# DeltaNet phase: the keys' norms from the diagonal of the key product, the values' convolution among the stages, the key-query product first

## Chip, cores and metric

The kernel runs on one core of a Trainium2 chip. The metric is the device time of one execution in microseconds (us). The engines are called PE (TensorE), DVE (VectorE), ACT (ScalarE), POOL (GpSimd) and SP (SyncE, which here only issues DMAs). Each engine works through its own instruction list; semaphores order the engines against each other. A difference under about 0.5% (9.6 us) can't be told from no change in a measurement of this kernel.

## What is computed

One layer of a hybrid encoder over 1024 prompt rows and 32 sample rows. The change lies wholly in mixer A, a gated delta rule over 8 heads. Cut to what matters:

```python
act = silu(causal_conv(u))                        # 4 taps, for q, k and v
q = l2norm(act_q) * DKA ** -0.5                   # x * rsqrt(sum(x * x) + 1e-6)
k = l2norm(act_k)
kk = einsum('nbhid,nbhjd->nbhij', kc, kc)
M = where(strict, beta * kk * decay_in, 0.0)      # decay_in = exp(G_i - G_j), 1 on the diagonal
sol = triangular_solve(M + eye, [beta * v, beta * exp(G) * k], lower=True)
qk = einsum('nbhid,nbhjd->nbhij', qc, kc) * decay_in
# then the recurrence over blocks: u = u_v - w_k S; o = q_dec S + qk u; S = S g_last + k_dec^T u
```

## The kernel before

The phases run one after the other: entry, DeltaNet (`phase_deltanet`, about 98 to 790 us of the trace), attention, merge, residual, dispatch, experts. Only the second is touched.

**Fill.** The projections of q, k, v and z (the gate) of all heads are products of the input with weights, each split into a high and a low part, so that a product is three matmuls (lines 142 to 144). One product of one head ("job") is 3 parts of 8 steps; a step is three matmuls. PE takes these steps as fill between the small products of the delta rule: `run(fill, n)` emits n of them. Weights of a job go through three engines: SP loads `wraw` (one buffer, so the DMA of job w waits for the split of job w-1), ACT makes the high part (`high`, line 625, right after it has taken the last part of a job), DVE (`low`, line 1065) or POOL (line 811) subtracts to get the low part. PE waits for the split at a job's first step.

**Order.** For h from -1 to 7 there is one pass of the loop, which works on two heads: the recurrence of head h, and the preparation of head a = h + 1. First come nine slots (one for each block of 128 rows of head h), then twelve stages, in the order of the tuple `A2`, for the inverse of the triangular matrix of head a. In a slot PE does the product of WE with the state S (line 1004), half of the slot's fill, the update with u (lines 1013 and 1014), the other half, and then a part of `prep(a)`. The DVE does u (line 1276), a part of its own `prep(a)`, S (line 1280), and another part. ACT does a part of its `prep(a)`, the evacuation of the block's output to `obuf`, and whatever products have become ready (`take`). Each `yield` in a `prep` ends a part. In pass -1 there is no recurrence.

**Fill steps.** Passes 0 to 5 have 96: 6 in each slot, 54 in all, then 3, 4, 3, 4, ... after the twelve stages. Passes -1 and 6 have 60 (5 and 4 in a slot). In passes 0 to 5 a job ends after 12, 36, 60 and 84 steps. In pass -1 it is after 24 and 48, in pass 6 after 12, 36 and 60.

**Preparation before** (slot numbers): PE: norms of the keys (`SK`: 18 matmuls of the squares with ones, 36 PE instructions, line 907) and key product (`KK`, line 865) in 2, norms of the queries (`SQ`) in 3, transposed decayed product (`T_ET`) in 4, transposed keys (`T_K`) in 7. ACT: tap 0 of the queries in 0, SiLU and square of the keys in 1, exponential of the decay matrix Dm in 2, SiLU and square of the queries in 3, square root and copies of the 32-wide diagonal blocks of ET to `blk` (line 692) in 4, tap 0 of the values in 5, keys and the block inverses RT and R in 8. DVE: taps 1 to 3 of the keys in 0, query taps in 1, 2 and 3, Dm in 1, `col` (1/norm of the keys, lines 1090 to 1094) and the split of one job's weights in 2, ET = KK * Dm in 3, transposition of the blocks in 4, scaling and N in 5, elimination (14 steps, lines 1051 and 1052) in 6 and 7, transposing back in 7, the three value taps (line 1033) in 8.

**Stages before**: BT, B, T_V (transposed values), B2, W, TT, T_O (output of head h), Q, QK (key-query product), TX, WK, UV. After each, `run(fill, ...)`. Some of the lines that matter:

```python
after_stage = {"BT": 2, "W": 3}        # DVE splits these jobs' weights behind these stages
# PE                                   # ACT, for i, stage in enumerate(A2):
if name == "B2":                       #   if stage == "B": evacuate_halves(a, "B", B)
    evacuated(pe, a, "BT")             #                    silu(a, VB)
    evacuated(pe, a, "B")              #   for k in range(subs_done(h, done), subs_done(h, now)):
    stage(a, "B2", mul2(A1T, B), HB2)  #       take(k)      # and high() behind a job's last part
```

Stage BT on PE waits for RT on ACT, which waits for the DVE's transposes of the blocks (semaphore `x_done`). B2 waits for the evacuations of BT (DVE) and B (ACT).

Of the kernel before, what the change touches and what calls it, by code (L numbers as in the profile page):

```python
# [17 lines left out]
ALU = mybir.AluOpType  # L18
# [379 lines left out]
def phase_deltanet(nc, c):  # L398
# [38 lines left out]
    A2 = ("BT", "B", "T_V", "B2", "W", "TT", "T_O", "Q", "QK", "TX", "WK", "UV")  # L437
# [26 lines left out]
    for h in range(-1, HA):  # L464
        a = h + 1
        order = ([] if a == HA else ["SK", "KK", "SQ", "T_ET", "T_K"]) + \
                [s for s in A2 if (a < HA or s == "T_O") and (h >= 0 or s != "T_O")]
        for s in order:
            for g in range(NGRP):
                if (s == "SK" and g != 0) or (s == "SQ" and g != 1):  # L470
                    continue
                use[h if s == "T_O" else a, s, g] = count[g]
                count[g] += 1

    with ExitStack() as ctx:
# [17 lines left out]
        A1T, Q, bv, sqk, sqq = UV[:, 0:TILES * HB2], UV[:, TILES * HB2:PAD], ET, kt, N  # L493
# [69 lines left out]
        with nc.Block() as block:  # L563
# [53 lines left out]
            def _(act):  # L617
# [35 lines left out]
                def tap(a, b):  # L653

                    act.wait_ge(s["pj_taken"], 2 + NJ * (jobs.index((a, b)) + 1))
                    if a > 0:
                        act.wait_ge(full[NGRP - 1], use[a - 1, "QK", NGRP - 1] + 1)
# [10 lines left out]
                def square(a, b):  # L668

                    act.wait_ge(s["actv"], 3 * a + (1 if b == KB else 2))  # L670
                    act.activation((sqk if b == KB else sqq)[:, :], f[b][:, :], ACT.Square).then_inc(s["sq"], 1)

                def prep(a):
# [4 lines left out]
                    square(a, KB)  # L678
# [16 lines left out]
                    yield  # L695
                    if a > 0:
# [62 lines left out]
                for h in range(-1, HA):  # L759
# [16 lines left out]
                    for i, stage in enumerate(A2):  # L776
                        if a < HA:
                            if stage == "B":
                                evacuate_halves(a, "B", B)
                                silu(a, VB)  # L780
                            if stage == "TT":
                                evacuate_corners(a)
                            if stage == "Q":
# [10 lines left out]
                            if stage == "QK" and a + 1 < HA:  # L794
# [41 lines left out]
            def _(pe):  # L836
# [63 lines left out]
                def norms(a, name, g, sq, n):  # L900

                    pe.wait_ge(s["sq"], 2 * a + n)
                    if use[a, name, g] > 0:
                        pe.wait_ge(free[g], use[a, name, g])
                    for t in range(TILES):
                        for rows in HALVES:
                            mm = pe.matmul(stg[g][rows, t:t + 1], tl(sq, t)[:, rows], c.consts[:, C_ONE, 0:1], start=True, stop=True)
                    mm.then_inc(full[g], 1)
# [1892 lines left out]
```

## Time and profile before

| | us |
|---|---|
| median of three runs | 1916.19 (1912.34 to 1922.93) |
| the profiled execution | 1919.02 |
| its span, first to last instruction | 1917.2 |
| PE busy, DVE busy, ACT busy | 1718.0, 1073.7, 768.4 |
| mean granted TensorE clock | 0.951 of 2.4 GHz |

The prediction uses the page's busy shares, the busy time by stretches, the table of who waited for whom, and the timeline. In the timeline a PE row's duration overlaps the next row's (matmuls are pipelined), so costs on PE are taken from start to start.

### The profile page before, as it was taken

The page shows a single profiled execution, that of the slowest core. Times are in us where ns is not written, and L with a number is a line of the kernel's source. Part 1 is how long each engine was busy: PE and PEld are TensorE (multiplying, and loading weights), DVE is VectorE, ACT ScalarE, POOL GpSimd, SP SyncE. Part 2 cuts the span into 40 slices and gives each one's busy share as a digit, 9 for nine tenths or more (in the row PEclk, how much of TensorE's full clock was granted, in tenths as well). Part 3 has the DMA queues.
Part 4 walks back from the last instruction along what each step waited for, and adds up shares of the span by engine and source line. Part 5 has one row for each costly group of instructions (what it writes and reads, how often), then busy time and mean ns, then how long its engine had stood idle before and what let it go on. Part 6 is the DMA issues. An engine that isn't in the chain of part 4 may idle for free. (4 is left out here: it accounts for less than half of the span.)

```text
span 1917.2 us, 32170 instructions
## 1 busy us (share of the span) xinstructions
PE 1718.0 (90%) x12253; PEld 1479.6 (77%) x12254; DVE 1073.7 (56%) x2257; ACT 768.4 (40%) x1473; POOL 150.5 (8%) x143
## 2 busy tenths in 40 slices
PE   5798999999999989899998899999979946999990
PEld 2597899999989989788884699998967834666660
DVE  5555747557584765354445211134349975677676
ACT  3455554645556454254444222222021113444444
POOL 0100000000000000000000000000000002434340
PEclk8898999999999999999999999999999966999995
DMA  9311021120202111212117321113153246988866
GB/s 335 136 60 49 23 74 38 49 73 14 74 23 75 37 49 39 94 40 81 57 70 275 124 68 67 45 57 100 34 176 144 110 172 231 320 258 287 230 186 214
DMA packets 69030, 219.80 MB, mean 115 GB/s; under 512 B 8580, under 2 KB 14364, under 8 KB 64804
## 3 DMA queue, kind: packets, MB, share of 16 engines
q1 hardware_dynamic: 61268, 190.20, 28.0%
q0 software_dynamic: 7632, 27.79, 5.9%
q8 instruction: 91, 1.49, 0.3%
q14 instruction: 39, 0.32, 0.1%
HBM read 178.11 MB, written 42.48 MB: 115 GB/s over the span
## 5 line engine op out<-in xcount | busy, mean ns | idle before, releaser
L142 PE MATMUL bk<-hT_high,w_high 128*128 128x352 f32 x840 | 294.5, 351 | 1.1 <-DVE ssq L1253 1.1
L144 PE MATMUL bk<-hT_high,w_low 128*128 128x352 f32 x840 | 271.6, 323 | 0.0
L143 PE MATMUL bk<-hT_low,w_high 128*128 128x352 f32 x840 | 271.4, 323 | 0.0
L142 PEld LDWEIGHTS bk<-hT_high,w_high 128*128 128x128 f32 x840 | 159.5, 190 | 5.3 <-DVE ssq L1253 1.2
L143 PEld LDWEIGHTS bk<-hT_low,w_high 128*128 128x128 f32 x840 | 159.8, 190 | 0.0
L144 PEld LDWEIGHTS bk<-hT_high,w_low 128*128 128x128 f32 x840 | 158.8, 189 | 0.0
L142 PE MATMUL pg<-hT_high,w_high 128*128 128x352 f32 x384 | 124.8, 325 | 5.8 <-PEq L1359 5.8
L143 PE MATMUL pg<-hT_low,w_high 128*128 128x352 f32 x384 | 123.8, 322 | 0.0
L144 PE MATMUL pg<-hT_high,w_low 128*128 128x352 f32 x384 | 123.7, 322 | 0.0
L1033 DVE SCALAR_TENSOR_TENSOR f<-raw,cw,f 128x1059 f32<-128x1059 f32 x72 | 97.0, 1348 | 9.3 <-ACT f L660 8.6
L2552 ACT ACTIVATE ws_high<-wgu 128x1024 fp32r x78 | 76.8, 1048 | 47.6 <-issue 44.0
L2617 DVE TENSOR_TENSOR ws_low<-wgu,ws_high 128x1024 fp32r<-128x1024 f32 x78 | 90.8, 1219 | 3.8 <-ACT ws_high L2552 2.0
L1276 DVE TENSOR_TENSOR u<-UV,bk 128x128 f32<-128x128 f32 x72 | 20.3, 282 | 124.1 <-PE bk L1004 123.6
L2529 PE MATMUL psD<-wdn,aTx 128*128 x192 | 87.1, 596 | 0.0
L2455 POOL TENSOR_TENSOR wait_cell<-wait_cell 128x1 f32<-128x1 f32 x27 | 19.7, 731 | 816.7 <-DVE idx L2593 816.7
L142 PEld LDWEIGHTS pg<-hT_high,w_high 128*128 128x128 f32 x384 | 72.7, 189 | 6.7 <-issue 6.7
L142 PE MATMUL psU<-ws_high,xs_high 128*128 128x512 f32 x150 | 67.1, 447 | 7.9 <-DVE xs_low L2608 4.7
L143 PEld LDWEIGHTS pg<-hT_low,w_high 128*128 128x128 f32 x384 | 72.8, 190 | 0.0
L144 PEld LDWEIGHTS pg<-hT_high,w_low 128*128 128x128 f32 x384 | 72.6, 189 | 0.0
L1497 ACT ACTIVATE pr<-sx,num 128x640 f32<-128x640 f32 (+5 forms) x72 | 50.6, 702 | 54.1 <-DVE num L1682 51.4
L1889 DVE TENSOR_TENSOR w_low<-wx,w_high 128x512 fp32r<-128x512 f32 (+1 forms) x32 | 18.6, 621 | 94.5 <-ACT w_high L1868 94.5
L142 PE MATMUL py<-wo_high,mix_high 128*128 128x512 f32 (+1 forms) x144 | 58.8, 409 | 12.1 <-DVE wo_low L2091 10.8
(464 smaller groups left out, 4134.7 us busy)
## 6 DMA issues: line engine op xcount, KB each, us to landing
wgu<-in_w_gu SPq DMA_DIRECT2D x16, 2048.0 KB, 10.6
wraw<-in_w_gdn SPq DMA_DIRECT2D x32, 512.0 KB, 3.6
wdn<-in_w_dn SPq DMA_DIRECT2D x16, 1024.0 KB, 14.7
wm<-in_w_mod SPq DMA_DIRECT2D x8, 1024.0 KB, 7.6
tmp_x<-x SPq DMA_DIRECT2D x16, 512.0 KB, 6.3
spare<-in_w_mod SPq DMA_DIRECT2D x12, 512.0 KB, 8.3
Dm<-tmp_g_rows SPq DMA_DIRECT2D x8, 576.0 KB, 6.0
EG<-tmp_g_rows SPq DMA_DIRECT2D x8, 576.0 KB, 7.0
```

The lines of the kernel that those rows point to most:

```text
L142: pe.matmul(out, lh, rh, start=start, stop=False)
L143: pe.matmul(out, lh, rl, start=False, stop=False)
L144: return pe.matmul(out, ll, rh, start=False, stop=stop)
L1033: ins = dve.scalar_tensor_tensor(out=f[b][:, 0:CONVW], in0=raw[b][:, k:k + CONVW], scalar=cw[:, a, b, k:k + 1], in1=f[b][:, 0:CONVW], op0= ...
L1276: dve.tensor_tensor(u[:, n % 2, :], tl(UV, n), sw[:, 0:P], ALU.subtract).then_inc(s["u"], 1)
L1497: act.activation(pr[tile(p, t) % 2][e][:, 0:nk], x[e][:, 0:nk], ACT.Exp, scale=SCALE, bias=num[:, e, 1:2], accum_out=num[:, e, 2:3]).then_ ...
L1889: dve.tensor_tensor(lo[:, half(j, h), :], raw[j % 2][:, half(j, h), :], plain(hi[:, half(j, h), :]), ALU.subtract).then_inc(w_split, 1)
L2455: pool.tensor_tensor(waits[:, 0:1], waits[:, 1:2], waits[:, 1:2], ALU.add).then_inc(pdone, 1)
L2529: mm = pe.matmul(psD[:, h * 512:(h + 1) * 512], aT[b][:, i, :], c.wdn[:, bass.ds(place, 1), i, h * 512:(h + 1) * 512].rearrange("p a c -> ...
L2552: act.activation(flat2(ws[b][0][:, PIECE * i:PIECE * (i + 1), :]), raw(place, i), ACT.Copy).then_inc(w_high, 1)
L2617: x = dve.tensor_tensor(flat2(low[:, part, :]), raw(place, i), plain(flat2(high[:, part, :])), ALU.subtract)
```

## The change

- The keys' norm is no longer a product of squares with ones on PE. The square of the keys on ACT and the `SK` product are gone. The DVE takes the norms from the diagonal of the 32-wide blocks of ET in `blk` (Dm is 1 there): a product with a mask (a new constant, identity of 32), a reduction over 32, then add, reciprocal and two products as before.
- On PE the key product moves to slot 1, `T_ET` to 3, `SQ` to 5. On ACT the copies to `blk` move to slot 3, SiLU and square of the queries to 4, the square root to 5. On the DVE, ET moves to the second part of slot 2, the weights' split to the second part of slot 3, `col` to slot 4, with the blocks' transposition behind it, the elimination has four parts in slots 6 and 7, and the back transposition is in slot 8.
- The value taps leave slot 8 and stand in stages QK, B and B2; `kd` moves from T_V to B; SiLU of the values from B to TT (ACT).
- The order of stages is QK, BT, B, B2, W, TT, T_O, Q, T_V, TX, WK, UV. The counts of fill steps by position are the same, and so are the stages' names behind which weights are split.
- The squares of the queries go to `kt` in place of `N`. ACT's tap 0 of the next keys moves from QK to Q.

```diff
-    A2 = ("BT", "B", "T_V", "B2", "W", "TT", "T_O", "Q", "QK", "TX", "WK", "UV")
+    A2 = ("QK", "BT", "B", "B2", "W", "TT", "T_O", "Q", "T_V", "TX", "WK", "UV")
...
                 def prep(a):                       # ACT
                     if a > 0:
                         tap(a, QB)
                     yield
                     silu(a, KB)
-                    square(a, KB)
                     yield
                     act.wait_ge(s["dm_min"], a + 1)
                     act.activation(Dm[:, :], Dm[:, :], ACT.Exp).then_inc(s["dm"], 1)
                     yield
-                    silu(a, QB)
-                    square(a, QB)
-                    yield
-                    act.wait_ge(s["cols"], a + 1)
-                    act.activation(col[:, 1, :], col[:, 0, :], ACT.Sqrt).then_inc(s["rk"], 1)
                     if a > 0:
                         act.wait_ge(s["r"], a)
                     evacuated(act, a, "KK")
...
                     x.then_inc(s["blk_in"], 1)
                     yield
+                    silu(a, QB)
+                    square(a)
+                    yield
+                    act.wait_ge(s["cols"], a + 1)
+                    act.activation(col[:, 1, :], col[:, 0, :], ACT.Sqrt).then_inc(s["rk"], 1)
                     if a > 0:
                         tap(a, VB)
...
                             if stage == "B":
                                 evacuate_halves(a, "B", B)
-                                silu(a, VB)
                             if stage == "TT":
                                 evacuate_corners(a)
+                                silu(a, VB)
...
                 def prep(a):                       # PE
                     yield
-                    yield
-                    norms(a, "SK", 0, sqk, 1)
                     pe.wait_ge(s["actv"], 3 * a + 1)
                     stage(a, "KK", mul(f[KB], f[KB]))
                     yield
-                    norms(a, "SQ", 1, sqq, 2)
                     yield
                     evacuated(pe, a, "KK")
                     stage(a, "T_ET", turn(ET))
                     yield
+                    yield
+                    norms(a)
...
                     dve.wait_ge(s["blk_in"], a + 1)          # DVE, slot 4
                     if a > 0:
                         dve.wait_ge(s["rt"], a)
+                    st.link(dve.tensor_tensor(blkT[:, :, :], blk[:, 0:TILES, :],
+                                              c.consts[:, C_M16, HB2:HB2 + BS].unsqueeze(1).to_broadcast([P, TILES, BS]), ALU.mult))
+                    st.link(dve.tensor_reduce(col[:, 0, :], blkT[:, :, :], AX.X, ALU.add))
+                    st.link(dve.tensor_scalar(col[:, 0, :], col[:, 0, :], L2_EPS, None, ALU.add))
+                    st.link(dve.reciprocal(col[:, 0, :], col[:, 0, :]))
+                    dve.tensor_tensor(c1[:, 0:TILES], tok(a, Q_NBETA), col[:, 0, :], ALU.mult)
+                    dve.tensor_tensor(col[:, 2, :], tok(a, Q_BEG), col[:, 0, :], ALU.mult).then_inc(s["cols"], 1)
+                    yield
                     dve.transpose(X[:, :, :], blk[:, :, :].rearrange("p t i -> p i t")).then_inc(s["x_raw"], 1)
...
-                    yield
-                    tap(a, VB, 1)
-                    tap(a, VB, 2)
-                    yield
-                    tap(a, VB, 3)
...
-                        if name == "T_V":
+                        if name in ("QK", "B", "B2"):
+                            tap(a, VB, 1 + ("QK", "B", "B2").index(name))
+                        if name == "B":
                             evacuated(dve, a, "T_K")
```

## Rows read from the trace of the kernel before

**Rows 1.** The page: busy time, share of the span, instructions.
```profile
PE 1718.0 (90%) x12253; PEld 1479.6 (77%) x12254; DVE 1073.7 (56%) x2257; ACT 768.4 (40%) x1473; POOL 150.5 (8%) x143
```

**Rows 2.** Busy time by stretch: length, PE, PEld, DVE, ACT, POOL, clock, DMA.
```profile
430.00:513.00 83.00, 80.65 (x773) 76.63 (x773) 54.12 (x118) 44.46 (x93) 2.86 (x3) 1.00 0.14 49
681.00:745.00 64.00, 56.00 (x592) 50.90 (x591) 51.60 (x115) 34.40 (x68) 0.47 (x2) 1.00 0.10 31
```

**Rows 3.** Who PE waited for, 90 to 800 us: total, times, longest.
```profile
PE bk L1013 <- DVE u L1276: 10.5, 17, 1.0
PE bk L868 <- ACT RT L706: 5.3, 1, 5.3
PE bk L907 <- ACT N L671: 4.7, 8, 1.4
PE bk L865 <- DVE col L1090: 2.9, 8, 0.4
```

**Rows 4.** Timeline of PE, passes 3 and 4: start, duration, line, what, count.
```profile
394.84 1.26 PE L868 MATMUL bk<-N,RT 64*64 64x64 f32 x36
...
397.58 0.32 PE L142 MATMUL bk<-hT_high,w_high 128*128 128x352 f32 x1
...
431.09 0.39 PE L1004 MATMUL bk<-S,WE 128*128 128x128 f32 x2
...
434.86 0.38 PE L1004 MATMUL bk<-S,WE 128*128 128x128 f32 x2
...
475.38 1.26 PE L868 MATMUL bk<-RT,N 64*64 64x64 f32 x36
```

**Rows 5.** Timeline of the DVE, then of ACT, in pass 3's stages.
```profile
394.66 1.35 DVE L1196 TENSOR_TENSOR yat<-obuf 128x1152 f32<-128x1152 f32 x1
396.04 1.23 DVE L1065 TENSOR_TENSOR w_low<-wraw,w_high 128x1024 fp32r<-128x1024 f32 x1
...
395.45 1.03 ACT L722 ACTIVATE WE<-bk 128x192 f32<-128x192 f32 x3 [1.46 <-PE bk L868]
...
400.78 1.06 ACT L625 ACTIVATE w_high<-wraw 128x1024 fp32r<-128x1024 f32 x1 [2.26 <-DMA wraw<-in_w_gdn]
```

**Rows 6.** Pass -1: timelines, two stretches, and the instructions on S.
```profile
119.31 0.21 ACT L666 ACTIVATE f<-f 128x32 f32<-128x32 f32 x1
...
146.53 0.48 DVE L1135 STREAM_TRANSPOSE blkT<-blk 128x288 f32<-128x288 f32 x1
...
148.90 2.00 PEld L868 LDWEIGHTS bk<-RT,N 64*64 64x64 f32 x36 [5.61 <-ACT RT L706]
...
148.00:150.00 2.00, 1.10 (x20) 1.10 (x22) 1.93 (x3) 1.94 (x5) 0.00 (x0) 0.50 0.00 0
...
158.00:160.00 2.00, 2.00 (x9) 1.62 (x7) 1.89 (x4) 0.00 (x0) 0.00 (x0) 0.50 0.00 0
...
L1004 PE MATMUL bk<-S,WE x128: 270/275/377, 180.8 to 780.8; 128*128 128x128 f32 x128
```

**Rows 7.** Timeline of PE, pass 6 and the start of pass 7.
```profile
681.23 0.39 PE L1004 MATMUL bk<-S,WE 128*128 128x128 f32 x2
...
722.79 1.26 PE L868 MATMUL bk<-RT,N 64*64 64x64 f32 x36
...
754.24 0.38 PE L1004 MATMUL bk<-S,WE 128*128 128x128 f32 x2
```

**Rows 8.** DVE operations, phase's groups: count, busy us, mean ns; taps: min/median/max.
```profile
L1033 DVE SCALAR_TENSOR_TENSOR f<-raw,cw,f x72: 1279/1317/2499, 94.0 to 723.8; 128x1059 f32<-128x1059 f32 x72
...
L1120 DVE TENSOR_TENSOR X<-X,c1c 128x256 f32<-128x256 f32 x16 | 6.0, 419 | 0.2 <-issue 0.2
L1135 DVE STREAM_TRANSPOSE blkT<-blk 128x288 f32<-128x288 f32 x8 | 3.8, 479 | 0.3
L1090 DVE TENSOR_SCALAR col<-bk 128x9 f32<-128x9 f32 x8 | 1.4, 169 | 23.8 <-PE bk L907 23.8
L1052 DVE TENSOR_TENSOR X<-X,prod 128x28 f32<-128x28 f32 (+6 forms) x112 | 27.4, 244 | 3.8
```

More of the change, by code:

```diff
@@ L465, in phase_deltanet @@
         a = h + 1
-        order = ([] if a == HA else ["SK", "KK", "SQ", "T_ET", "T_K"]) + \
+        order = ([] if a == HA else ["KK", "T_ET", "SQ", "T_K"]) + \
                 [s for s in A2 if (a < HA or s == "T_O") and (h >= 0 or s != "T_O")]
@@ L656, in tap @@
                     if a > 0:
-                        act.wait_ge(full[NGRP - 1], use[a - 1, "QK", NGRP - 1] + 1)
+                        last = "T_V" if b == VB else "QK"
+                        act.wait_ge(full[NGRP - 1], use[a - 1, last, NGRP - 1] + 1)
                         if b == QB:
@@ L793, in _ @@
                                 evacuate(a, "UV", UV)
-                            if stage == "QK" and a + 1 < HA:
+                            if stage == "Q" and a + 1 < HA:
                                 tap(a + 1, KB)
@@ L898, in turn, with norms @@
                     return lambda t, out: pe.transpose(out, tl(m, t), c.consts[:, C_ID, :])
[L900 to L904, printed above, removed]
+                def norms(a):
+                    pe.wait_ge(s["sq"], a + 1)
+                    pe.wait_ge(free[1], use[a, "SQ", 1])
                     for t in range(TILES):
                         for rows in HALVES:
-                            mm = pe.matmul(stg[g][rows, t:t + 1], tl(sq, t)[:, rows], c.consts[:, C_ONE, 0:1], start=True, stop=True)
-                    mm.then_inc(full[g], 1)
+                            mm = pe.matmul(stg[1][rows, t:t + 1], tl(sqq, t)[:, rows], c.consts[:, C_ONE, 0:1], start=True, stop=True)
+                    mm.then_inc(full[1], 1)
                 def prep(a):
                     yield
-                    yield
-                    norms(a, "SK", 0, sqk, 1)
                     pe.wait_ge(s["actv"], 3 * a + 1)
@@ L1088, in prep @@
                     yield
-                    src = take_from(dve, a, "SK", 0)
-                    dve.tensor_scalar(col[:, 0, :], src[:, 0:TILES], L2_EPS, None, ALU.add).then_inc(free[0], 1)
-                    dve.wait_ge(free[0], use[a, "SK", 0] + 1)
-                    st.link(dve.reciprocal(col[:, 0, :], col[:, 0, :]))
-                    dve.tensor_tensor(c1[:, 0:TILES], tok(a, Q_NBETA), col[:, 0, :], ALU.mult)
-                    dve.tensor_tensor(col[:, 2, :], tok(a, Q_BEG), col[:, 0, :], ALU.mult).then_inc(s["cols"], 1)
-                    if first_job[a - 1] + 1 in in_slots:
-                        low(first_job[a - 1] + 1)
-                    yield
-                    tap(a, QB, 3)
-                    yield
                     dve.wait_ge(s["dm"], a + 1)
@@ L1103, in prep @@
                         dve.tensor_tensor(grp(ET, g), src[:, 0:W3], grp(Dm, g), ALU.mult).then_inc(free[g], 1)
[L1104 to L1105 removed]
                     yield
[L1107 to L1109 removed]
+                    tap(a, QB, 3)
+                    yield
+                    if first_job[a - 1] + 1 in in_slots:
+                        low(first_job[a - 1] + 1)
                     yield
```

27 lines of the change are left out of this document (14 added, 13 removed).

## The prediction

> **What bounds the kernel now.** I read the page's busy shares first: TensorE (PE) 90%, VectorE (DVE) 56%, ScalarE (ACT) 40% [rows 1]. The change touches only the DeltaNet phase, about 98 to 790 us, so next come the stretches of it: PE is busy 80.7 of 83 us in a full head pass and 56 of 64 in the last one that prepares a head [rows 2]. PE executes a fixed list there, hence a gain is either an instruction taken off PE or a wait of PE that goes. The wait table names the waits: for the DVE's u and S in the recurrence, for the square and for col around the norms, and 5.3 us in one piece for RT [rows 3]. That busy time hides small gaps (ends are modelled), so I take starts from the timeline.
>
> I call a head pass the time from slot 0 of head h to slot 0 of h+1 and name it by h. Passes 0 to 5 have 96 fill steps, pass -1 and pass 6 have 60.
>
> **A full pass before.** Pass 4: slot 0 at 431.09, slot 1 at 434.86, so an undisturbed slot is 3.77; the first stage starts at 475.38, slots 44.3 us [rows 4]. Work in them: 9 x 3.77 = 33.9, the key product 2.1, two norms of 1.15 each, two transposes of 1.0: 40.3. So about 4.0 are waits. Of these 0.2 to 0.6 each are before the two norms (square), 0.4 before the key product (col), and the rest in slots 5 to 8, where between two states the DVE runs elimination (224 small operations over eight heads of 0.24 us, about 7.8 us a head with their links), transposes and value taps [rows 3, 8].
>
> **Slots after.** SK goes: -1.15. The key product needs the SiLU only, with no square and no col ahead. The square of the keys (1.17 on ACT) covers nothing and leaves ACT room. The DVE gives three taps (1.3 each, [rows 8]) to the stages and gets the diagonal's chain in slot 4. No row shows a masked multiply and reduce over 288 elements; bounds are 0.38 to 0.42 (256 elements, [rows 8]) and 0.48 (288 elements in transpose, [rows 8]) apiece. I take 0.41 plus 0.04 for the link, near the first; with add 0.2, reciprocal 0.25, two overlapping small products 0.17 (a small operation has 0.17, [rows 8]) the chain is 1.5 (1.4 to 1.7). It lies between u and S of slot 4, where DVE otherwise idles about 1.5 for PE. Its input, blk, is copied by ACT in slot 3 (four copies, 1.8), done about 3 us earlier. DVE per slot is then 4.4, 4.1, 3.1, 2.9, 4.2, 3.5, 4.5, 4.3 for slots 0 to 7, together 31.0, against 35.3 on PE (3.77 each, key product in slot 1, ET's transpose in 3, query norm in 5, key transpose in 7). u and S may each come 1.5 late without a PE wait, and walking the slots one by one I find none. Slots: 39.1, that is **-5.2** per full pass. If half of the old waits stay it is -3.2.
>
> **Stages after.** They take 39.05 before (from 475.38 and the same pass), with no waits. I count from the key-query product, T = 0. Three engines decide it:
> - PE: QK 1.9, three fill steps, BT from 3.5 to 4.7 (1.19), then four steps of 0.48. The fill changes to the next weights after step 60. Slots take 54, first stage 3, so that is the fourth step of the second stage, at T = 6.2. Before it was the fourth after B: low part split at 396.04 + 1.23 = 397.27, PE there at 397.58 [rows 4, 5]. It was just in time.
> - DVE: QK combine to 2.7, value tap to 4.0, BT's evacuation to 5.1, the square of obuf 1.35 + link to 6.5, the split 1.23 to 7.7 (the last two as at 394.66 and 396.04, [rows 5]). So the QK combine and a tap now stand ahead of the split: **PE waits 1.5**.
> - ACT: in the stage named BT it takes the finished product and then makes the high part of the weights after next. Their DMA waits for this split, and lands 3.5 after it (397.27 to ACT's start at 400.78, which was 2.26 of idling, [rows 5]). So ACT stands until T = 11.25 and is done at 12.3. B's evacuation is queued behind it, to 13.35. Before it stood ahead of it (395.45, [rows 5]) because B was the stage in which this product ended. B2 on PE needs it; PE would be there at T = 11.1: **another 2.3**.
> After that W's combine ends at 18.9, PE needs it at 19.4; TT, T_O, Q, values, TX, WK, UV follow with margins of 1 to 5 us. Stages: 39.05 + 3.85 = 42.9. A full pass is thus -5.2 + 3.85 = **-1.3**, and six of them -8.
>
> The trace shows ACT doing nothing else while it idles for that DMA [rows 5]; the order is its instruction list's. If ACT could take B's evacuation first, the second wait would go, and the sum would be 6 x 2.3 = 14 lower. The Trainium skill, "TensorE: Matmul & The Clock Gate", Part 1 (engine queue depths), says that ScalarE and VectorE are strict first-in first-out; that speaks against the change, and by it the sum stays as it is. The trace agrees: in that idle time ACT takes nothing from behind.
>
> **Pass -1.** No recurrence, so the DVE chain decides. x_done came at 147.0 (146.53 + 0.48), BT at 148.90 when RT was there, after 5.6 idle on PE, and the clock was then 0.50, 1.2 GHz, against 1.00 in a full pass [rows 2, 6]. After: SiLU of the keys at 119.5 [rows 6], product (2.1) to 121.6, ET (exponential at 122.4, then 1.4) to 123.9, third query tap, split and chain (1.3 + 1.2 + 1.5) to 127.9, transpositions (2.3) to 130.2, scaling and N (3.0) to 133.2, elimination 7.9 to 141.1, two transposes (2.5): 143.6, i.e. 3.4 earlier, chiefly since ET no longer queues behind the square and SK. QK fills 2.4 us of PE in front of BT; BT starts at 145.5 with 1.6 idle. B2 follows at 149.0 (160.0 before) since the values' transpose, its SiLU and 2.5 us idle are no longer between them and the clock is full. Small waits then: W 0.7, TT 0.4, values 0.4. Slot 0 of head 0 starts at 169.4 against 180.8 [rows 6]: **-11.3**. Should the clock fall all the same, -7; the lower bound is -12.
>
> **Pass 6.** Four steps per slot: PE needs 2.81, DVE is the bound. Slots ran 681.23 to 722.79, 41.6 [rows 7]. Walked as above with the DVE's new parts I get 33.9: -7.7 (taps -3.9, SK and its three waits, less the chain). Stages took 31.45 (to 754.24, [rows 7]); here the weights change lies later, and only the DVE's taps push: W waits 1.4, TT 1.8, against about 2.3 of waits and gaps there before: +0.9. **-6.8** (-4 to -8). Pass 7 has neither preparation nor the moved stages: 0.
>
> **At nothing**: the split in slot 3 in place of slot 2 (needed only for slot 5's DMA and slot 6's product, 8 us away). The cover of that move is the gate's product on PE (24 steps); with it gone, the 1.2 of the split would count in each pass, 7 us in all. The weights' DMAs move with their splits: in SP's queue each waits for the split before it, and only the one that follows BT's split has a reader close behind. The row DMA for the next head's decays waits for the QK combine, which now comes earlier.
>
> **Sum.** -11.3 - 8 - 6.8 = -26. The profiled execution took 1919.0 with a span of 1917.2 and lies 2.8 over the median of three, 1916.2, inside their spread. From its own time: 1893. From the median, which I forecast: **1890**.
>
> **Rivals.**
> 1. The stage waits don't come, as DMA or DVE are quicker than I walk: then -5.2 + 0.4 in six passes, -29, total -47: 1869. For: the split missed PE by only 1.5. Against: the first-in order of ACT and 3.5 of DMA are in rows. 12%.
> 2. Slots gain only half (waits re-form as u and S are late in slots 6 to 8, where DVE has 4.5 against 3.77): six passes at +0.7, pass 6 -4, -11 in the first: -11: 1905; with pass -1's clock fallen, 1909. 17%.
> 3. Slower: in each full pass the two new waits (1.5 and 2.3 us) drop the granted clock as the idle time of pass -1 did [rows 6]. B2, W, TT and their fill, 9 us at full speed, then run at 1.2 GHz: up to +9 each. It decides from +4.5 a pass, where six passes eat the 26. At +7: 1890 + 42 = 1932. For: in pass -1 the clock was at 0.50 once more at 158 to 160, right after a wait of PE for the values' SiLU [rows 6]. Against: pass 6 has 8 us of idle time in 64, in many pieces, and kept 1.00 [rows 2]. The Trainium skill, "TensorE: Matmul & The Clock Gate", Part 1, says that the halved clock is the default state and that activity releases it; the fall in pass -1 agrees. 9%.
> 4. The change does little: the new order moves the waits rather than ends them, net within 9 us, e.g. because ACT's three table loads land before the exponential in slot 2 (it has 0.4 to spare): 1910. 12%.
> Forecast as walked, 1880 to 1902: 50%.
>
> **Range and chances.** About 0.5% (9.6 us) is what a measurement of this kernel can tell from no change. Faster: forecast, rival 1, over half of 2, a little of 4: 0.72. Within: 0.18. Slower: 0.10. The range 1868 to 1911 takes in rival 1 and most of 2 and 4, and leaves out rival 3. It is not narrower, as the two waits per pass carry +-3 us six times.
>
> **What would show it.** Right: 144 matmuls' instructions of the key norm gone; slots of a full pass 39 to 40; in the stages a PE wait at the fourth fill step after BT and one before B2, ACT idle for wraw and B's evacuation behind it; BT in pass -1 near 145.5 at clock 1.00; pass 6 about 7 shorter. Wrong: u or S still late in slots 6 to 8; no wait before B2; a clock below 1.00 in the full passes.

## The result, and the profile after

The changed kernel takes 1900.08 us (median of four, 1896.21 to 1903.03) against 1917.85 (1912.34 to 1922.93) for the kernel before. The medians are 17.8 us or 0.9% apart; the ratio on record is 0.9887, 95% interval 0.986 to 0.9914, that is 1.1% faster. (1917.85 is the median of the three executions in the table ahead of the prediction and one more.) The forecast was 1890, the range 1868 to 1911. The profiled execution took 1903.03 with a span of 1901.0 and a mean granted clock of 0.951, as before.

One slip of numbering in the prediction and in the titles of rows 4 and 5: counted by its own rule, the pass that starts at 431.09 is pass 3, and the stages shown around 395 are those of pass 2. Nothing else hangs on it. Below, passes are numbered -1 to 7 by the recurrence's head.

The page after, busy time, share and instructions, for [rows 1]: PE has 17 us and 288 instructions less, the 36 of the norm's product in each of eight heads.

```profile
PE 1700.8 (89%) x11965; PEld 1470.3 (77%) x11966; DVE 1083.4 (57%) x2273; ACT 759.0 (40%) x1465; POOL 151.6 (8%) x143
```

Who PE waited for in the changed kernel, 90 to 800 us (total, times, longest), for [rows 3]:

```profile
PE bk L868 <- ACT WE L722: 13.9, 6, 4.0
PE bk L142 <- DVE w_low L1063: 8.1, 6, 1.3
PE bk L906 <- DVE N L1056: 3.4, 7, 0.9
PE bk L1011 <- DVE u L1273: 2.1, 4, 1.0
...
PE bk L868 <- ACT RT L706: 0.9, 1, 0.9
```

The 5.3 for RT is down to 0.9, u from 17 waits to 4, the waits for the square and for col are gone. Three new ones stand on top: B2 for B's evacuation (line 722), the fill for its low part (L1063), each in all six full passes as predicted, and the query norms for N, which was not.

Read from the PE timeline, start to start, in us (a position is counted from its pass's slot 0; the first stage is BT before and QK after):

| | before | after |
|---|---|---|
| slot 0 of head 0 | 180.77 | 168.33 |
| full passes 0 to 5, length | 83.54, 83.4 (five) | 84.12, 84.16, 82.62, 86.04, 84.45, 82.65 |
| first stage at | 44.3 | 39.83 |
| B2 at | 52.9 | 53.1; 55.16 in pass 3; 53.4 in pass 4 |
| from B2 to W | 3.3 | 3.3 in passes 2 and 5; 4.69 to 4.86 in 0, 1, 3, 4 |
| pass 6 | 73.01 | 68.32 |

Slot 0 of head 0 comes 12.4 us earlier, but not all of that is the change's. A product of constants with `PT`, which stands ahead of everything that was changed, came 0.83 earlier in this execution (first line before, second line after):

```profile
90.96 0.38 PE L983 MATMUL bk<-consts,PT 128*72 128x128 f32 x2
...
90.13 0.38 PE L981 MATMUL bk<-consts,PT 128*72 128x128 f32 x2
```

Over the traces of all the runs below, this product starts between 89.0 and 91.5. From it to slot 0 of head 0 it is 89.81 us before and 78.16 to 78.21 in every trace with the whole change, so this distance is what can be compared: pass -1 brought 11.6 us. Pass 6 brought 4.7, and the six full passes, where a gain of 8 was expected, cost 3.6. The nine slots of a full pass did get shorter by 4.5 together, and the stages gave most of it back: 3.75 in each pass, and in four of them 1.5 more, in pass 3 another 2.1.

PE's timeline in the stages of pass 2 (start, duration, line, what, count, idle time before and who ended it), a pass without the extra loss, for [rows 4]:

```profile
384.23 0.43 PE L142 MATMUL bk<-hT_high,w_high 128*128 128x352 f32 x1 [1.34 <-DVE w_low L1063]
384.91 1.26 PE L868 MATMUL bk<-N,RT 64*64 64x64 f32 x36
389.74 1.26 PE L868 MATMUL bk<-WE,UV 64*64 64x64 f32 x36 [1.93 <-ACT WE L722]
393.04 1.26 PE L868 MATMUL bk<-UV,WE 64*64 64x64 f32 x36
```

The DVE there: the combine (L1141), the value tap (L1031), BT's evacuation and the square stand ahead of the split (L1063), which ends at 384.17, and PE starts at 384.23.

```profile
377.97 1.23 DVE L1141 TENSOR_TENSOR PT<-bk,Dm 128x384 f32<-128x384 f32 x2
379.12 1.31 DVE L1031 SCALAR_TENSOR_TENSOR f<-raw,cw,f 128x1059 f32<-128x1059 f32 x1
380.59 1.06 DVE L1154 TENSOR_TENSOR UV<-bk,consts 128x192 f32<-128x192 f32 x3 [0.16 <-PE bk L868]
381.56 1.35 DVE L1193 TENSOR_TENSOR yat<-obuf 128x1152 f32<-128x1152 f32 x1
382.95 1.22 DVE L1063 TENSOR_TENSOR w_low<-wraw,w_high 128x1024 fp32r<-128x1024 f32 x1
```

And ACT in the same stages, for [rows 5]: it stands 4.11 us for the DMA of the weights, and B's evacuation, which before came ahead of that, follows 0.96 behind. B2 starts 0.26 after it.

```profile
387.77 1.06 ACT L625 ACTIVATE w_high<-wraw 128x1024 fp32r<-128x1024 f32 x1 [4.11 <-DMA wraw<-in_w_gdn]
388.73 0.75 ACT L722 ACTIVATE WE<-bk 128x192 f32<-128x192 f32 x3
```

Pass 3 has the same waits, the second with 3.96 in place of 1.93, and the slow clock on top: the distance from B2 to W is 4.69. The first line is the query norms' wait for N, which every full pass has in slot 5.

```profile
445.49 1.22 PE L906 MATMUL bk<-consts,kt 128*64 128x1 f32 x36 [0.42 <-DVE N L1056]
...
474.39 2.19 PE L868 MATMUL bk<-WE,UV 64*64 64x64 f32 x36 [3.96 <-ACT WE L722]
479.08 1.26 PE L868 MATMUL bk<-UV,WE 64*64 64x64 f32 x36
```

Busy time by stretch (length, PE, PEld, DVE, ACT, POOL, clock, DMA share and GB/s), right behind B2 in passes 0, 1 and 2, then pass 6. In passes 0 and 1 the granted clock is 0.50, or 1.2 GHz; in pass 2 it is 1.00.

```profile
222.00:224.00 2.00, 2.00 (x32) 1.88 (x29) 1.11 (x4) 0.48 (x1) 0.00 (x0) 0.50 0.00 0
...
307.00:309.00 2.00, 2.00 (x8) 2.00 (x8) 2.00 (x3) 0.00 (x0) 0.00 (x0) 0.50 0.00 0
...
391.00:393.00 2.00, 2.00 (x13) 1.82 (x12) 2.00 (x4) 0.00 (x0) 0.00 (x0) 1.00 0.00 0
...
672.00:740.00 68.00, 62.43 (x630) 58.33 (x629) 52.99 (x119) 36.56 (x76) 0.47 (x2) 1.00 0.10 29
```

The new chain on the DVE, of which [rows 8] had no row, in pass -1: from the first of its operations to the transposition behind it, at 126.91, it is 1.6 us.

```profile
125.31 0.45 DVE L1100 TENSOR_TENSOR blkT<-blk,consts 128x288 f32<-128x288 f32 x1
125.80 0.45 DVE L1102 TENSOR_REDUCE col<-blkT 128x9 f32<-128x288 f32 x1
126.29 0.17 DVE L1103 TENSOR_SCALAR col<-col 128x9 f32<-128x9 f32 x1
```

### The profile page after: what moved, and what is told of

The parts are those of the page before. It is cut to its first block and busy times, and to the rows that moved or that the text cites. A ratio compares the mean times of both kernels' runs of the same rounds, so it can differ in the third digit from the quotient of the medians.

```text
span 1901.0 us, 31602 instructions
## 1 busy us (share of the span) xinstructions
PE 1700.8 (89%) x11965; PEld 1470.3 (77%) x11966; DVE 1083.4 (57%) x2273; ACT 759.0 (40%) x1465; POOL 151.6 (8%) x143
## 5 line engine op out<-in xcount | busy, mean ns | idle before, releaser
L1031 DVE SCALAR_TENSOR_TENSOR f<-raw,cw,f 128x1059 f32<-128x1059 f32 x72 | 97.1, 1348 | 9.0 <-ACT f L661 8.6
L142 PE MATMUL py<-wo_high,mix_high 128*128 128x512 f32 (+1 forms) x144 | 58.1, 404 | 11.3 <-DVE wo_low L2088 10.1
```

The lines of the kernel that those rows point to most:

```text
L142: pe.matmul(out, lh, rh, start=start, stop=False)
L1031: ins = dve.scalar_tensor_tensor(out=f[b][:, 0:CONVW], in0=raw[b][:, k:k + CONVW], scalar=cw[:, a, b, k:k + 1], in1=f[b][:, 0:CONVW], op0= ...
```

## The experiments

**Theory**, as it stood before the experiments. Each full pass loses 3.75 us to two in-order queues. DVE: the key-query combine and a value tap stand ahead of the weights' split, so PE waits 1.35. ACT: B's evacuation stands behind `high`, which stands for the DMA that waits for that split, so PE waits 1.9. In four passes the second wait also drops PE's clock, for 1.5. **Rivals:** the clock is the main cost and the waits cover one another, so that removing one brings little; or the DVE's work as a whole bounds the stages, and the waits move when one is taken away. A third question is which part of the change brings its gain.

### ACT's queue: the high part behind B's evacuation

Only ACT's order changes: the high part that is due in stage BT is made after B's evacuation, in the six full passes.

```diff
-                    if j == NJ - 1:
+                    if j == NJ - 1 and not hold:
                         high(i // NJ + 2)
...
                                 evacuate_halves(a, "B", B)
+                                if held:
+                                    high(held.pop())
...
-                            take(k)
+                            wait = stage == "BT" and a < HA and k % NJ == NJ - 1
+                            take(k, wait)
+                            if wait:
+                                held.append(k // NJ + 2)
```

> The changed kernel with one move on ScalarE: in stage BT it takes the finished product, but makes the high part of the weights after next only behind B's evacuation. Queue theory (B's evacuation stands behind a wait for the weights' DMA): the wait before B2 (13.9 us in six passes) goes, the 1.35 us wait for the split stays, the clock has no second gap to fall in; six full passes give back 12 us and up to 8 us of slow clock: 1880 to 1888 us. Rival, the value taps make VectorE the bound of the stages: W or TT waits for VectorE instead and the time stays within 4 us of the changed kernel (1900).

Measured: 1884.3 us (1880.82 to 1887.83), kernel before 1922.84 beside it, ratio 0.9804 (0.9782 to 0.9826). Each full pass is 80.63 and B2 stands at 51.13. Its PE timeline, pass 1: 2.83 from B to B2, 3.31 from B2 to W, and no wait but that for the split.

```profile
295.48 0.43 PE L142 MATMUL bk<-hT_high,w_high 128*128 128x352 f32 x1 [1.34 <-DVE w_low L1069]
296.16 1.27 PE L874 MATMUL bk<-N,RT 64*64 64x64 f32 x36
298.99 1.26 PE L874 MATMUL bk<-WE,UV 64*64 64x64 f32 x36
302.30 1.26 PE L874 MATMUL bk<-UV,WE 64*64 64x64 f32 x36
```

This is inside the 1880 to 1888 expected. B2 comes 2.0 earlier than in passes 2 and 5 of the changed kernel, all six passes are alike, and the wait for the split is unchanged (8.1 in six). The queue on ACT is shown as the cause, and that the slow clock hung on this wait. The DVE is no bound here: the stages simply got shorter.

### The DVE's queue: the split ahead of the value tap, BT's evacuation and the square

```diff
                             combine(a, "QK", PT, Dm, ALU.mult)
+                        if name == "QK" and h < HA - 2:
+                            low(first_job[h] + 2)
                         if name in ("QK", "B", "B2"):
...
                 def stage_low(h, name):
+                    if h < HA - 2 and name == "BT":
+                        return
```

> The changed kernel with one move on VectorE: in passes -1 to 5 the split of the next weights stands behind the key-query combine and ahead of the first value tap, not behind BT and the square of the outputs. Queue theory: the split ends about 3.9 us after the start of the key-query product, 2.3 us before TensorE wants it, its successor's DMA lands near 7.5 and ScalarE is free at 8.5, so both waits go (8 + 14 us) and with them the slow clock of four passes (about 8 us): 1870 to 1880 us. Rival, VectorE is the bound of the stages: BT's evacuation and W's combine come later by 1.2 us, new waits of 1 to 2 us in each pass appear, 1890 to 1900 us.

Measured: 1875.17 us (1872.89 to 1883.02), ratio 0.9759 (0.9728 to 0.979). Full passes 79.03, 79.98, then 79.02 four times. Its waits of PE, 90 to 800 us: the split's line is gone, and B2's wait is down from six times to one of 0.9.

```profile
...
PE bk L906 <- DVE N L1056: 3.4, 7, 0.9
PE bk L1011 <- DVE u L1277: 1.7, 3, 1.0
...
PE bk L868 <- ACT WE L722: 0.9, 1, 0.9
```

One edit on the DVE ends both waits, since the DMA starts 3.83 us earlier with the split (43.74 in place of 47.57 within the pass) and ACT no longer stands long for it. The two waits were one chain: split, DMA, high part, evacuation. A pass is 3.6 us shorter than the two of the changed kernel that kept the clock (82.6): that is the price of the loop, a little more than the two waits on the page. The value tap and the square of obuf, pushed back by 1.1 and 0.7 us, cost nothing. The edit moves the split past three things at once, the tap, BT's evacuation and the square; which of them mattered is settled further below, by the order of stages alone.

### Idle time filled: 16 and 8 products without use ahead of B2

The waits stay; PE is kept at work in the second one, by products of constants into an unused part of PSUM, in the six full passes. The second kernel has `FILLERS = 8`.

```diff
+    FILLERS = 16
...
                     if name == "B2":
+                        for _ in range(FILLERS if 0 <= h < HA - 2 else 0):
+                            pe.matmul(sw[:, 384:512], c.consts[:, C_ID, :], c.consts[:, C_ONE, :], start=True, stop=True)
                         evacuated(pe, a, "BT")
```

> The changed kernel with 16 products of constants (128 columns each, about 1.7 us together) in front of TensorE's wait before B2 in passes 0 to 5, written to unused columns; nothing reads them. They do no work of the reference. Clock theory (the halved clock costs about 1.5 us in four of six passes): the idle time is filled, the granted clock stays 1.00 there, and the kernel gets 4 to 8 us faster although TensorE has more to do. Rival, the lower clock is not due to the idle time or costs nothing: same time, or slower by up to 6 us.

Measured: 1903.44 us (1899.63 to 1904.81), ratio 0.9892 (0.987 to 0.9914). All six passes are 84.2 and B2 to W takes 3.30 in each, so the clock held. But the gain of 4 to 8 us did not come: the 16 products took 3.7 us, not the 1.7 put down for them, and so lasted longer than the wait. B2 stands at 54.71 and not at 53.1. What the clock gave back, the filler took, and the time is what the rival had said. Hence the half dose, which takes 1.95:

> As the kernel with 16 filler products, but 8 of them (about 1.8 us), which end before B's evacuation does. They do no work of the reference. Clock theory: B2 starts 53.1 us into each full pass as in the changed kernel, its following stages run at clock 1.00 in all six passes, each pass takes 82.7 us, together 7 to 9 us less than the changed kernel. Rival, passes 2 and 5 kept the clock by chance and filling changes nothing: passes of 82.6 to 86 us as before, same time.

Measured: 1899.82 us (1892.92 to 1905.67), ratio 0.9891 (0.9854 to 0.9929). The same stretches in its trace as in pass 0 above, and in pass 4:

```profile
222.00:224.00 2.00, 2.00 (x42) 1.93 (x39) 1.51 (x4) 0.84 (x1) 0.00 (x0) 1.00 0.04 8
554.00:556.00 2.00, 2.00 (x23) 1.78 (x23) 2.00 (x2) 0.00 (x0) 0.00 (x0) 1.00 0.00 0
```

B2 is at 53.0 to 53.24, B2 to W takes 3.30 in all six, and the passes are 82.52 to 82.73. So the fall of the clock cost 1.5 us in each of four passes, 6 us in all. The six passes together are 8.3 shorter than in the changed kernel's trace; the other 2.3 are a longer load of the weights in pass 3 and a little in pass 4, which didn't occur here. Only the trace resolves this: the changed kernel beside it took 1903.51, 3.7 more where 7 to 9 were expected, and the two intervals of the ratio overlap. The rival that the clock is the main cost falls: the two waits without the clock cost 3.6 x 6, against 6 for the clock.

### The order of stages alone

The kernel before with the key-query product first; T_V stays where it was.

```diff
-    A2 = ("BT", "B", "T_V", "B2", "W", "TT", "T_O", "Q", "QK", "TX", "WK", "UV")
+    A2 = ("QK", "BT", "B", "T_V", "B2", "W", "TT", "T_O", "Q", "TX", "WK", "UV")
...
-                        act.wait_ge(full[NGRP - 1], use[a - 1, "QK", NGRP - 1] + 1)
+                        act.wait_ge(full[NGRP - 1], use[a - 1, "T_V" if b == VB else "QK", NGRP - 1] + 1)
...
-                            if stage == "QK" and a + 1 < HA:
+                            if stage == "Q" and a + 1 < HA:
                                 tap(a + 1, KB)
```

> The kernel before with the key-query product as first stage and nothing else moved but what that needs (the values' transpose stays between B and B2; ScalarE's tap 0 of the next keys moves to Q). Queue theory: the two new waits come with this order alone, and the first of them now stands before the values' transpose, whose SiLU is queued behind B's evacuation: plus 4 to 6 us in each of six full passes, while pass -1 gains 2 to 4 us: 1935 to 1950 us. Rival, the waits come from the value taps in the stages: passes 0 to 5 as in the kernel before, 1912 to 1918 us.

Measured: 1957.42 us (1953.1 to 1962.12), ratio 1.0174 (1.0145 to 1.0203): the slowest of all, and 7 over the range expected. Full passes are 87.9 to 91.7, where 87.4 to 89.4 had been expected. Passes 0, 3 and 5 lie within that (87.85 to 88.3); in passes 1, 2 and 4 the granted clock fell to 0.50 during the wait of T_V, and in pass 1 the load of the weights took 5.1 us as well. Its waits of PE, 90 to 800 us:

```profile
PE bk L898 <- ACT f L666: 20.8, 8, 4.3
...
PE bk L142 <- DVE w_low L1065: 8.1, 6, 1.3
PE bk L868 <- DVE PT L1146: 5.6, 1, 5.6
```

The split's wait is the one of the changed kernel to the tenth, so it belongs to the order of stages, and neither to the norms nor to the value taps: here the taps are still in slot 8, and the rival that the waits come from them falls. The DVE's timeline, in a full pass, shows why:

```profile
405.79 1.48 DVE L1146 TENSOR_TENSOR PT<-bk,Dm 128x384 f32<-128x384 f32 x3
407.99 1.06 DVE L1159 TENSOR_TENSOR UV<-bk,consts 128x192 f32<-128x192 f32 x3 [0.72 <-PE bk L868]
408.97 1.35 DVE L1196 TENSOR_TENSOR yat<-obuf 128x1152 f32<-128x1152 f32 x1
410.35 1.23 DVE L1065 TENSOR_TENSOR w_low<-wraw,w_high 128x1024 fp32r<-128x1024 f32 x1
```

Without the tap the DVE just stands 0.72 longer for BT's product; with it, in the changed kernel, it still stood 0.16. In both, the split starts 2.97 behind BT's start, after BT's evacuation and the square, and ends at 4.2. In the kernel before it ended later, 5.3 behind BT's start, but PE came for it only 5.6 behind. With BT as the second stage PE comes 2.9 behind it. So what stood in the split's way was BT's evacuation and the square, and the tap ran in time that was free.

The same loop on ACT now delays the values' SiLU as well, which is queued in B behind the evacuation, and T_V waits for it (20.8). Pass -1 gains nothing, where 2 to 4 were expected: slot 0 of head 0 is at 179.61, but the product with `PT` had started at 89.13, so it is 90.5 us from there, 0.7 more than before.

### The preparation alone

The norms from the diagonal and their new places in the slots, with the old order of stages; value taps in slot 8, SiLU of the values in B.

```diff
-    A2 = ("QK", "BT", "B", "B2", "W", "TT", "T_O", "Q", "T_V", "TX", "WK", "UV")
+    A2 = ("BT", "B", "T_V", "B2", "W", "TT", "T_O", "Q", "QK", "TX", "WK", "UV")
...
                                 evacuate_halves(a, "B", B)
+                                silu(a, VB)
...
                                 evacuate_corners(a)
-                                silu(a, VB)
...
+                    yield
+                    for k in range(1, CW):
+                        tap(a, VB, k)
...
-                        if name in ("QK", "B", "B2"):
-                            tap(a, VB, 1 + ("QK", "B", "B2").index(name))
-                        if name == "B":
+                        if name == "T_V":
                             evacuated(dve, a, "T_K")
```

> The changed kernel with the old order of stages, the value taps back in slot 8 (behind the back transposition), kd in T_V and SiLU of the values in B: the preparation's part of the change alone. Part theory: slots of a full pass shrink as in the changed kernel (39.8), BT waits about 1 us for RT, the wait for the split and the one before B2 don't exist, clock 1.00: full passes 79 to 81 us against 83.4, pass -1 gains 3 to 5 us, pass 6 gains 3 to 5: 1890 to 1900 us, as good as the changed kernel. Rival: the old order lets BT, B and the values' transpose wait for taps that now come later (2 us or more a pass), and the gain of the slots is lost: 1905 to 1920 us.

Measured: 1894.62 us (1890.93 to 1896.4), kernel before 1919.59 beside it, ratio 0.9872 (0.9847 to 0.9896): at least as good as the whole change (0.9912, 0.9888 to 0.9936, on the same chip). Full passes are 80.76, 2.6 under before; the stages take 39.3, within 0.2 of before. Their slots take 41.47, not 39.8, since in every pass BT now waits for RT:

```profile
PE bk L868 <- ACT RT L706: 15.0, 8, 3.2
...
PE bk L906 <- DVE N L1056: 3.4, 7, 0.9
```

The wait is 1.5 in a full pass, where 1 had been expected. That is what the key-query product ahead of BT covers in the changed kernel. Pass -1 gains 4.4, counted from the product with `PT` (at 89.46), within the 3 to 5 expected; pass 6 gains 2.3, less than the 3 to 5 expected.

### Both queues mended, and the query norms one slot later

Both edits above, and PE's `norms(a)` with the DVE's use of them one slot later, past N.

```diff
                     yield
                     yield
+                    yield
                     norms(a)
-                    yield
                     yield
...
-                        if j == 7:
+                        if j == 10:
                             src = take_from(dve, a, "SQ", 1)
```

> The changed kernel with the split ahead of the first value tap, the high part behind B's evacuation, and the query norms one slot later (slot 6, their evacuation in the first part of slot 7), so that they need not wait for the off-diagonal blocks. If the three are what is left of waits in a full pass: 78.6 us in each, none longer, 2 to 6 us below the kernel with the split alone, 1868 to 1875 us. Rival, the norms in slot 6 push slot 7's state or VectorE's evacuation of them stalls the elimination: slots of 39.8 or more and no gain over the split alone.

Measured: 1873.46 us (1871.19 to 1875.74), ratio 0.9762 (0.9736 to 0.9788), 2.4% under the kernel before. The time can't be told from that of the kernel with the split moved (0.9759), so the gain of 2 to 6 us over it isn't shown by the time. The trace has the full passes at 78.55 as expected, against 79.02, and pass 6 at 67.11. What is left of PE's waits for this phase, 90 to 800 us, longest first, none of it in a full pass:

```profile
...
PE bk L1017 <- DVE u L1283: 2.0, 4, 1.0
PE bk L874 <- DVE UV L1152: 1.3, 1, 1.3
...
```

The wait for N is gone, and it was worth 0.47 in a full pass and 1.1 in the slots of pass 6 (first stage at 34.09, against 35.23 in the changed kernel).

### The changed kernel once more

> The changed kernel again, as the neighbour on the same chip for the other three. By its trace four of six full passes lose 1.5 us or more to the slower clock, by where the wait falls; if that is a matter of chance, other passes lose it here, and the number of them differs, 1893 to 1905 us. Rival, the program fixes it: the same passes 0, 1, 3 and 4.

Measured: 1903.51 us (1901.79 to 1909.53), ratio 0.9912 (0.9888 to 0.9936). Full passes 84.25, 84.01, 82.7, 85.98, 84.24, 82.52. The clock fell in the same four full passes, and pass 3 was again the long one, as the rival had said. But this is weaker than it looks. Read with fine windows, the granted clock fell 53.2, 54.4, 54.9 and 54.2 us into passes 0, 1, 3 and 4 in the first trace, and at 53.2, 54.3, 54.9 and 54.2 in this one: the two executions were nearly one case twice, and none with other moments was traced. And in pass 6 they differ (first line the changed kernel, second its repetition, both 25 us into the pass):

```profile
697.00:699.00 2.00, 2.00 (x16) 2.00 (x15) 1.76 (x9) 0.39 (x2) 0.00 (x0) 1.00 0.00 0
...
698.00:700.00 2.00, 2.00 (x9) 2.00 (x9) 1.45 (x7) 0.00 (x0) 0.00 (x0) 0.50 0.00 0
```

So the same program has a fall in one execution and none in the other at the same place. Whether the four passes are fixed by the program stays open.

### Pass -1: the clock without the change

The kernel before, with 23 such products on PE ahead of BT in pass -1, where it idled 5.6 us and the clock fell [rows 6].

```diff
+    FILLERS = 23
...
                     if name == "BT":
+                        for _ in range(FILLERS if h < 0 else 0):
+                            pe.matmul(sw[:, 384:512], c.consts[:, C_ID, :], c.consts[:, C_ONE, :], start=True, stop=True)
                         pe.wait_ge(s["rt"], a + 1)
```

> The kernel before with 23 products of constants (about 5.2 us) in front of TensorE's wait for RT in pass -1 and nowhere else. They do no work of the reference. BT starts at 148.9 as before. Clock theory (a part of the 12.5 us that pass -1 gained is the clock that no longer falls behind that idle time): the clock stays 1.00 from 149 to 154, and head 0's slot 0 starts 3 to 6 us earlier than at 180.8. Rival, the stages of pass -1 hang on ScalarE and VectorE whatever TensorE's clock: 180 to 181.

Measured: 1919.67 us over ten executions against 1924.12 over thirteen of the kernel before, ratio 0.9983 (0.9961 to 1.0005), not to be told from no change. In the trace BT starts at 148.13 with 0.32 of wait left, and slot 0 of head 0 at 177.2. The product with `PT` came 0.93 earlier than in the trace before, which is all of BT's 0.8 and a part of slot 0's 3.6. From that product it is 2.6 less to slot 0, and from BT's start 2.8: about 2.7 us is what the clock had cost in pass -1, a little under the 3 to 6 expected, while the rival, no gain, falls. A stretch ahead of T_V (at 154.67) in which PE has little to do stays at 1.00:

```profile
148.13 1.26 PE L869 MATMUL bk<-RT,N 64*64 64x64 f32 x36 [0.32 <-ACT RT L707]
...
152.00:155.00 3.00, 0.76 (x6) 0.47 (x5) 0.17 (x2) 2.59 (x4) 0.00 (x0) 1.00 0.49 173
```

Two more things stand in this trace, whose passes 0 to 6 run the very instructions of the kernel before. In pass 4 the load of the weights took 5.0 us from the split in place of 3.3 to 3.7, and the pass is 83.38 like its neighbours: with B's evacuation ahead of ACT's high part, this late load cost nothing. And pass 6 took 74.61 against 73.01, with the granted clock at 0.50 from 21 us into it, where the kernel before had kept 1.00.

## Why the prediction was right, and where it wasn't

- **Slots of a full pass: -5.2 expected, -4.45 measured** (44.3 to 39.83). Missing was the wait of the query norms for N, 0.42 (later shown worth 0.47). The step that failed is "walking the slots one by one I find none": u and S were walked, but not the squares' product, which had moved from slot 3 to slot 5, right behind the DVE's scaling and N. The other 0.3 is the work itself: in the kernel with all three edits no wait is left in a full pass, and its slots take 39.36 where 39.1 was added up.
- **The diagonal's chain on the DVE: 1.5 expected (1.4 to 1.7), 1.6 measured**: 0.45 in place of 0.41 for each of the two operations over 288 elements. It lies at no wait of PE.
- **Stages: +3.85 expected, +3.75 measured** in passes 2 and 5. Split wait 1.35 for 1.5, B2's 1.9 for 2.3, B2 at T = 13.3 for 13.4. The wait at B2 was taken away by itself (2.0 came back), the split's together with it (3.6). One reason given was wrong: "the QK combine and a tap now stand ahead of the split". The order of stages alone has the same 1.35 with no tap there; in the way are BT's evacuation and the square, while PE comes for the split 2.9 us behind BT's start instead of 5.6. The Trainium skill, "TensorE: Matmul & The Clock Gate", Part 1, as cited, holds: B's product was done, but its evacuation did not overtake the high part in the 4.11 us for which ACT stood.
- **Clock.** Rival 3's mechanism came true at a fraction of its price: in four of six passes, 1.5 us each, not up to 9. The forecast as walked had the full passes at full clock. The stretch at 1.2 GHz ended before W, as B2 to W took 4.8 in place of 3.3 and everything from W on was at its old distances. What was mis-sized is the length of the stretch, taken from pass -1 where idle pieces followed one another. It costs 6 us of the 11.6 by which the full passes missed their sum.
- **A longer DMA.** In pass 3 the load took 5.6 us from the split to ACT's start, where the others took 3.5 to 3.8. As ACT's queue hangs on it, that went to PE one for one: 2.1. In the kernel before ACT stood for this load as well [rows 5], but B's evacuation was done by then.
- **Full passes together: -8 expected, +3.6 measured.** This is the term that was mis-sized, by 11.6: slots 4.5, clock 6, DMA 2.1, less 1 for stages a little better than sized.
- **Pass -1: -11.3 expected, -11.6 measured**, once the 0.83 is taken off by which the whole phase had started earlier. BT starts at 144.66, or 145.5 with that correction, as expected; it waits 0.89 for RT, and the clock stays at 1.00. By itself, the order of stages loses 0.7 here and the preparation brings 4.4, so 7.9 us come only with both. The clock accounts for some 2.7 us of the 11.6.
- **Pass 6: -6.8 expected, -4.7 measured.** Slots 35.2 for 33.9 expected: the query norms wait 0.92 for N, and moving them brought 1.1. The rest lies in the stages, 33.1 for 32.35: W waits 1.13 and TT 1.26, less than the 1.4 and 1.8 expected, so the old waits and gaps that I took off against them, 2.3 us, were set too high. In the trace before, PE's waits there are 0.26 and 0.33.
- **Sum: -26 expected, -17.8 measured** by medians, -16.2 by the spans of the two traces. Of these 16.2, 0.83 came ahead of the phase, 12.7 between there and slot 0 of head 7 (11.6 - 3.6 + 4.7), and 2.65 behind it, where nothing was changed. That last part took 1160.3 us in this trace and 1165.1 in the repetition of the same kernel, so it is not the change's. In the repetition the changed part gained 12.4. So the changed part gained less than half of the 26 forecast. That the time still fell inside the range is owed to the range's width, and in part to luck: 3.5 of the 16.2 us came from outside the phase.

Was the whole order needed? The two parts alone make a full pass 5.7 slower and 2.6 faster, together 3.1 slower; jointly they make it 0.6 slower. They do help each other, but with the waits in place the order of stages is worth nothing beyond the preparation. With the split moved ahead, it is: 79.02 a pass against 80.76.

## What to carry to other kernels

When a stage is moved, list for each engine what then stands ahead of every operation that another engine, or a DMA, waits for; here an evacuation and a square ahead of a split cost 3.6 us a pass over a loop of three queues (split, DMA, high part, evacuation), and moving that one split brought the time from a ratio of 0.989 to 0.976, about as much again as the change itself had. Not everything in the list counts: the tap ran while the DVE would have stood for PE anyway. A DMA's reader should be queued behind all that is due meanwhile, since then a transfer that is 1.5 us late costs nothing (5.1 us in pass 3 with ACT's queue mended, at 80.64 a pass like the rest). When two traces are compared by position, first check where a product that stands ahead of the change has come to lie: here that was 0.8 us of 12.4, and in one run it made a gain of 1.2 out of a loss of 0.7. And after the long wait is gone, walk again each product that was moved, not only those that were critical before.

## What was not expected of the hardware

- **The clock falls in some of equal passes.** With the same instructions and the same waits (1.35, then 1.9 us, 5.5 us apart), the clock fell in passes 0, 1, 3 and 4 and not in 2 and 5, in both traces of the changed kernel. The Trainium skill, "TensorE: Matmul & The Clock Gate", Part 1, says that the moment of the change varies between runs of one kernel; in pass 6 it did, with a fall in one of the two traces and none in the other, and in the full passes the two traces agree. Eight products of constants in the wait held the clock in all six.
- **One load in some is longer.** The loads of 512 KB behind BT's split took 3.3 to 3.8 us, but 5.6 in pass 3 of the changed kernel, 5.5 in pass 3 of its repetition, 5.1 in pass 3 with ACT's queue mended, 4.7 in pass 5 with 16 fillers, 4.8 in pass 1 with the split moved, 5.1 in pass 1 with the order of stages alone and 5.0 in pass 4 of the kernel before with fillers in pass -1; with 8 fillers, with the preparation alone and in the kernel before none was. What it meets there stays open. It is also why pass 1 with the split moved took 79.98.
- **DVE and POOL take turns.** In pass -1 a product of two SBUF tensors took 3.06 us, with the same shape 1.35 elsewhere. It had started while POOL's split of weights ran (2.36 us from 152.19), and ended 1.2 us after that did:

```profile
152.71 3.06 DVE L1180 TENSOR_TENSOR kt<-kt,col 128x1152 f32<-128x1152 f32 x1
```

All eleven traces agree on this, 90 to 800 us. 42 of the DVE's value, key and query taps and of its products into `kt`, `kd` and `yat` over 1152 elements overlap a split on POOL. In 40 of them POOL had started first, and they took 2.4 to 3.1 us. The other 1013 of these shapes, beside which no split ran, took at most 1.36. The 2499 ns of the longest tap in [rows 8] are of this kind. In the remaining two, one each in the kernel with the split moved and in the one with all three edits, the DVE had started first, by 0.06 us. There the DVE's operation kept its time, and POOL's split took 3.5 in place of 2.4:

```profile
151.15 1.31 DVE L1031 SCALAR_TENSOR_TENSOR f<-raw,cw,f 128x1059 f32<-128x1059 f32 x1
...
151.21 3.48 POOL L811 TENSOR_TENSOR w_low<-wraw,w_high 128x1024 fp32r<-128x1024 f32 x1 [20.36 <-ACT w_high L625]
```

So in these traces whichever started second took longer. The DVE's updates of S, which read one input from PSUM, kept their 0.35 us beside POOL's split. No run took POOL's work away.
